# Even layer: products of gates and convolution in 128-column pieces between the steps of its two attentions

## What is computed

```python
q_blocks = jnp.moveaxis(qa.reshape(B, nb, Q_BLOCK, A_HEADS, 2, A_QK), 1, 0)
o = lax.map(lambda qb: diff_attend(qb, k_all, v_all, lam), q_blocks)   # p0 - lam * p1, 768 keys
...
out_a = diff_attention_post(o, subln, lam_init).astype(px.dtype) * jax.nn.silu(ga)
out_b = short_conv(bb, cb, ub, conv_w) * jax.nn.silu(gb)               # b * conv3(c * u)
out_x = jnp.concatenate([out_a, out_b], axis=-1)
...
oc = diff_attend(qc.reshape(B, L, A_HEADS, 2, A_QK), kc, vc, lam)      # context: 256 keys
```

## Time and profile before

| | us |
|---|---|
| median of three runs (lowest, highest) | 1628.0 (1619.35, 1629.15) |
| profiled execution, its own time | 1629.48 |
| its span | 1627.7 |
| busy: PE, DVE, ACT, POOL | 1428.6, 743.7, 661.2, 433.1 |
| attention d, first score to last dc copy | 795.8 to 980.1 |
| first e_ga product to last gc product | 988.5 to 1162.7 |

### The profile page before, as it was taken

One profiled execution on the slowest core, in us unless ns is written; L12 is line 12 of the kernel. 1 busy time (PEld: TensorE's weight loads), 2 busy tenths in 40 slices (PEclk: granted clock), 3 DMA queues, 4 the chain that ended last, 5 costly groups with the idle time before them and its releaser, 6 DMA issues. The chain is left out here.

```text
span 1627.7 us, 20847 instructions
## 1 busy us (share of the span) xinstructions
PE 1428.6 (88%) x7788; PEld 1145.8 (70%) x7788; DVE 743.7 (46%) x1455; ACT 661.2 (41%) x1426; POOL 433.1 (27%) x340
## 2 busy tenths in 40 slices
PE   5999789999999788599899879999795898889986
PEld 4777567776787566586677757888684786777765
DVE  2154875644314222604499887322303603982123
ACT  4435226643422333421477662411224423663323
POOL 2433243430343323122100002323131333112522
PEclk9999899999999899799999989999998899999998
DMA  4212242100333534320000001121222210103341
GB/s 160 85 71 78 104 156 78 53 27 27 130 130 128 195 110 149 117 95 35 26 1 1 2 1 52 52 78 53 85 84 107 87 75 26 47 24 138 122 151 56
DMA packets 23250, 129.98 MB, mean 80 GB/s; under 512 B 2544, under 2 KB 4208, under 8 KB 10608
## 3 DMA queue, kind: packets, MB, share of 16 engines
q1 hardware_dynamic: 16304, 106.10, 18.0%
q10 hardware_dynamic: 6848, 22.55, 3.9%
HBM read 122.35 MB, written 6.29 MB: 79 GB/s over the span
## 5 line engine op out<-in xcount | busy, mean ns | idle before, releaser
L930 POOL TENSOR_TENSOR w_low<-w_raw,w_high 128x512 fp32r<-128x512 f32 x296 | 384.6, 1308 | 1112.7 <-ACT w_high L1017 1112.5
L1017 ACT CAST w_high<-w_raw 128x512 fp32r<-128x512 f32 x296 | 179.2, 620 | 667.9 <-PE psum L564 490.8
L564 PE MATMUL psum<-x_high,w_high 128*128 128x512 f32 (+1 forms) x696 | 285.1, 410 | 18.1 <-DVE k_low L1615 8.9
L564 PE MATMUL psum<-x_low,w_high 128*128 128x512 f32 (+1 forms) x696 | 275.0, 395 | 0.0
L564 PE MATMUL psum<-x_high,w_low 128*128 128x512 f32 (+1 forms) x696 | 274.2, 394 | 0.0
L564 PEld LDWEIGHTS psum<-x_high,w_high 128*128 128x128 f32 (+1 forms) x696 | 132.3, 190 | 59.6 <-issue 26.8
L679 PE MATMUL psum<-k_high,q_masked 128*128 128x256 f32 (+3 forms) x512 | 139.2, 356 | 31.4 <-DVE q_masked L1609 15.6
L564 PE MATMUL psum<-w_high,x_high 128*128 128x512 f32 (+1 forms) x352 | 140.5, 399 | 20.0 <-ACT w_high L1017 12.7
L564 PEld LDWEIGHTS psum<-x_high,w_low 128*128 128x128 f32 (+1 forms) x696 | 131.7, 189 | 30.1
L564 PEld LDWEIGHTS psum<-x_low,w_high 128*128 128x128 f32 (+1 forms) x696 | 132.4, 190 | 21.9 <-issue 0.5
L564 PE MATMUL psum<-w_low,x_high 128*128 128x512 f32 (+1 forms) x352 | 137.8, 391 | 0.0
(11 more groups left out here) (262 smaller groups left out, 2468.3 us busy)
## 6 DMA issues: line engine op xcount, KB each, us to landing
w_raw<-stream SPq DMA_DIRECT2D x98, 1024.0 KB, 4.8
x_kept<-arena ACTq DMA_DIRECT2D x8, 512.0 KB, 4.3
arena<-x_kept ACTq DMA_DIRECT2D x8, 512.0 KB, 6.5
arena<-bias ACTq DMA_DIRECT2D x8, 448.0 KB, 3.3
arena<-rows ACTq DMA_DIRECT2D x6, 512.0 KB, 5.3
arena<-x SPq DMA_DIRECT2D x4, 512.0 KB, 5.2
arena<-x ACTq DMA_DIRECT2D x4, 512.0 KB, 6.0
arena<-ctx ACTq DMA_DIRECT2D x4, 512.0 KB, 4.9
```

The source lines that it names most:

```text
L564: mm = pe.matmul(o, l, r, start=(first and n == 0 and kind != "fc"), stop=(last and n == len(passes) - 1))
L930: pool.tensor_tensor(WL[:, u % ROOM, :], RAW[:, g % 2, u % 4, :], WH[:, u % ROOM, :].bitcast(F32), ALU.subtract).then_inc(w_lo, 1)
L1017: act.copy(WH[:, u % ROOM, :], RAW[:, g % 2, u % 4, :]).then_inc(w_hi, 1)
```

## The change

The five chunks after e_v become 20 slim ones of 128 columns, in the order gate, c, u, b, last gate for each of four column blocks; each is two units, with four k of 128 rows in one unit. `slim` makes a chunk in 16 pieces: eight k for x (three 128x512 matmuls each, bank 6), then eight k for the context (three 128x256 matmuls, bank 7). The two attentions run in one loop over 48 steps on each engine, with four calls of `feed_even` per step, which lay 320 pieces over the first 45 steps, one or two at a time. All transposes use bank 4, all value products bank 5. What ACT and DVE do with a finished chunk stands in their `fed_even`, one step behind PE. The square means come after the loop, and each attention tile is scaled and gated at once. The rows of `w_out` are rolled by 512, so that eo0 starts with the convolution's half. In `dc` ACT now copies out all transposes, where DVE copied half.

```diff
+SLIM = ("e_gate", "e_c", "e_u", "e_b", "e_last")
...
+    + [("e_q", 8), ("e_k", 8), ("e_v", 8)] + [(f"{part}_{j}", 2) for j in range(4) for part in SLIM]
...
+    chunks |= halves("eo", np.roll(a["w_out_2"][0], -512, axis=0)) | halves("oo", a["w_out_2"][1]) | {"dft": dft}
     stream = np.zeros((4 * N_GRANULES, P, 512), f)
     for name, units in UNITS.items():
...
                     for k in range(len(UNITS[chunk])):
                         yield from tiles(chunk, k, X)
+            def slim(chunk):
+                units = UNITS[chunk]
+                for part, x in enumerate((X, C)):
+                    key = (chunk, part)
+                    acc = open_bank(key, 6 + part)
+                    for k in range(NK):
+                        u = units[k // 4]
+                        pe.wait_ge(w_hi, u + 1)
+                        pe.wait_ge(w_lo, u + 1)
+                        w = slice(P * (k % 4), P * (k % 4) + P)
+                        wh, wl = WH[:, u % ROOM, w], WL[:, u % ROOM, w]
+                        hi, lo = x[k]
+                        o = acc[:, 0:hi.shape[-1]]
+                        for n, (l, r) in enumerate(((wh, hi), (wh, lo), (wl, hi))):
+                            mm = pe.matmul(o, l, r, start=k == 0 and n == 0, stop=k == NK - 1 and n == 2)
+                        if k == NK - 1:
+                            fills_bank(mm, key)
+                            closed.append(key)
+                            if part:
+                                unit_done[u] = (bank_full[fills[key][0]], fills[key][1] + 1)
+                        elif part and k == 3:
+                            used[0] += 1
+                            mm.then_inc(w_used, 1)
+                            unit_done[u] = (w_used, used[0])
+                        yield
...
                     next(pieces, None)
                 new = set(unit_done) - before
                 fed[phase].append(max(new) if new else (fed[phase] or [-1])[-1])
+                while closed:
...
             keys = lambda pr, w: (KH[:, pr, 0:w], KL[:, pr, 0:w])
-            attention("d", keys, *pv)
-            attention("dc", keys, *pv)
...
+                    mm = pe.transpose(acc[:, P * (kt - c):P * (kt - c) + P],
+                                      E_P[:, 2 * (i % 2), P * kt:P * kt + P], ident)
+                fills_bank(mm, key)
...
+            pieces = (piece for j in range(4) for part in SLIM for piece in slim(f"{part}_{j}"))
+            n_pieces, n_feeds = 4 * len(SLIM) * 2 * NK, 4 * (len(EVEN) - 3)
+            def feed_even():
+                n = len(fed["e"])
+                feed("e", pieces, n_pieces * (n + 1) // n_feeds - n_pieces * n // n_feeds if n < n_feeds else 0)
+            for s in range(len(EVEN) + 3):
+                if s < len(EVEN):
+                    score_two(s, 0)
+                feed_even()
+                if s < len(EVEN):
+                    score_two(s, 1)
+                feed_even()
+                if 1 <= s <= len(EVEN):
+                    turn_two(s - 1, 0)
+                feed_even()
+                if 1 <= s <= len(EVEN):
+                    turn_two(s - 1, 4)
+                if s >= 3 and s % 2:
+                    values_two((s - 3) // 2)
+                feed_even()
+            for n, i in enumerate(TILE_ORDER):
+                pe.wait_ge(sig("sq"), n + 1)
                 acc = next_bank(("ms", i))
                 fills_bank(pe.matmul(acc[:, :], square("ones_blk"), E_SQ[:, i, :], start=True, stop=True),
                            ("ms", i))
-            for chunk in ("e_ga", "cb", "ub", "bb", "gc"):
-                gemm(chunk, X, C)
             gate_rows(0)
-            mixed = [(BH[:, k, :], BL[:, k, :]) for k in range(4)] + X[4:]
-            mixed_c = [(KH[:, k, 0:L], KL[:, k, 0:L]) for k in range(4)] + C[4:]
+            mixed, mixed_c = X[4:] + X[:4], C[4:] + C[:4]
             gemm("eo0", mixed, mixed_c, ready=lambda k: pe.wait_ge(sig("mix_lo"), 3 * (k // 2) + 3))
             gemm("eo1", mixed, mixed_c)
...
+            def fed_even(s):
+                for chunk, part in closed_in("e", s):
+                    name, j = chunk[:-2], int(chunk[-1])
+                    if name in ("e_gate", "e_last", "e_c"):
+                        ps = filled(act, (chunk, part))[:, 0:L if part else S]
+                    if name == "e_gate":
+                        act.activation((E_GC if part else E_G)[:, j, :], ps, ACT.Sigmoid).then_inc(sig("e_gate_sig"), 1)
+                    if name == "e_last":
+                        if j:
+                            act.wait_ge(sig("e_conv_done"), 2 * j - 1 + part)
+                        act.activation((E_WC if part else E_W)[:, :], ps, ACT.Sigmoid).then_inc(sig("e_last_sig"), 1)
+                    if name == "e_c":
+                        if j:
+                            act.wait_ge(sig("e_conv_in_read"), 2 * j - 1 + part)
+                        frees(act.copy((E_ZC if part else E_Z)[:, :], ps), (chunk, part))
+            for hh in range(2):
...
+            for s in range(len(EVEN) + 3):
+                if s:
+                    high((fed["e"] + [fed["e"][-1]] * 8)[4 * s - 1] + ROOM)
+                exps_even(s, 0)
+                if 2 <= s < len(EVEN) + 2:
+                    turned_even(s - 2, 4)
+                if s:
+                    fed_even(s - 1)
+                if 1 <= s <= len(EVEN):
+                    turned_even(s - 1, 0)
...
+            act.wait_ge(sig("e_conv_done"), 8)
+            high_mixed([(XH[:, 4 + j, :], E_Y[:, j, :]) for j in range(4)],
+                       [(CH[:, 4 + 2 * p:6 + 2 * p, :], E_YC[:, 2 * p:2 * p + 2, :]) for p in range(2)], lambda n: None)
+            ahead("e_last_3")
+            for i in TILE_ORDER:
                 ps = filled(act, ("ms", i))
...
+            def fed_even(s):
+                for chunk, part in closed_in("e", s):
+                    name, j = chunk[:-2], int(chunk[-1])
+                    key, w = (chunk, part), L if part else S
+                    g, y = (E_GC[:, j, :], E_YC[:, j, :]) if part else (E_G[:, j, :], E_Y[:, j, :])
+                    z, last_gate = (E_ZC[:, :], E_WC[:, :]) if part else (E_Z[:, :], E_W[:, :])
+                    if name == "e_c":
+                        continue
+                    ps = filled(dve, key)[:, 0:w]
+                    if name == "e_gate":
+                        dve.wait_ge(sig("e_gate_sig"), 2 * j + part + 1)
+                        frees(dve.tensor_tensor(g, g, ps, ALU.mult), key)
+                    if name == "e_u":
+                        consumed(dve, (f"e_c_{j}", part))
+                        frees(dve.tensor_tensor(z, z, ps, ALU.mult), key)
+                        consumed(dve, key)
+                        convolve(j, z, y, w)
+                    if name == "e_b":
+                        dve.wait_ge(sig("e_conv_in_read"), 2 * j + part + 1)
+                        frees(dve.tensor_tensor(y, y, ps, ALU.mult), key)
+                    if name == "e_last":
+                        consumed(dve, (f"e_b_{j}", part))
+                        dve.wait_ge(sig("e_last_sig"), 2 * j + part + 1)
+                        frees(dve.tensor_tensor(last_gate, last_gate, ps, ALU.mult), key)
+                        consumed(dve, key)
+                        dve.tensor_tensor(y, y, last_gate, ALU.mult).then_inc(sig("e_conv_done"), 1)
...
+                max_even(s, 0)
+                if 1 <= s <= len(EVEN):
+                    name, i = EVEN[s - 1]
+                    of_even(name, norm_d, norm_dc)(i, ATT[name].tile(i))
+                if s:
+                    fed_even(s - 1)
+                max_even(s, 1)
+                for name, first, preps in (("d", 0, preps_d), ("dc", ATT["d"].steps, preps_dc)):
...
+                        preps(*ahead_by)
+                if s - ATT["d"].steps in (-2, -1):
+                    preps_dc(0, s - ATT["d"].steps + 2)
+            dve.wait_ge(sig("e_conv_done"), 8)
...
-            for i, v in enumerate(values):
-                dve.tensor_tensor(E_SQ[:, i, :], v, v, ALU.mult).then_inc(sig("sq"), 1)
-            for i, v in enumerate(values):
+            for i in TILE_ORDER:
+                dve.tensor_tensor(E_SQ[:, i, :], values[i], values[i], ALU.mult).then_inc(sig("sq"), 1)
+            gains = [E_G[:, j, :] for j in range(4)] + [E_GC[:, 2 * p:2 * p + 2, :] for p in range(2)]
+            for i in TILE_ORDER:
                 consumed(dve, ("ms", i))
-                r = E_RS[:, i, :]
+                r, v = E_RS[:, i, :], values[i]
                 link(dve.reciprocal(r, r))
-                dve.scalar_tensor_tensor(v, v, scr(83), r, ALU.mult, ALU.mult).then_inc(sig("subln"), 1)
-            dve.wait_ge(sig("subln"), 6)
+                link(dve.scalar_tensor_tensor(v, v, scr(83), r, ALU.mult, ALU.mult))
+                v = v if i < 4 else pair(v)
+                dve.tensor_tensor(v, v, gains[i], ALU.mult).then_inc(sig("e_gated"), 1)
```

(14 more changed lines are left out.)

181 lines of the change are left out of this document (120 added, 61 removed), and 1 row of the table STREAM.

## The result

The changed kernel takes 1665.97 us (median of 4 runs, 1664.92 to 1667.68), the kernel before 1627.18 (4 runs, 1619.35 to 1629.15): ratio 1.0247, 95% interval 1.0228 to 1.0267. The forecast was 1641 with a range up to 1664. The change makes the kernel slower by 2.5%, nearly three times as much as forecast. Its profiled execution took 1667.68 us, its span 1665.9.

The account below looks back on a forecast made before the run. DVE's chain bounds the attentions, PE the chunks. Work 297.3, interleaving 9.2, transposes 11.6, banks 16.0, other waits 4.5, end 10.5 make a 349.1 us loop; with a 47.0 us tail PE restarts 13 us later: 1641 us, range 1611 to 1664.

Parts of the forecast that it names:

- The tail: Between the loop's last copy and PE's restart: 47.0 us, 22.5 more than before, as reciprocals now stand ahead of eo0.
- Banks 6 and 7: In the loop, a chunk's first piece waits until its bank is read out: 16.0 us (bounds 5 and 25).
- work at full clock: PE's work in the loop, d 114.6, fed dc steps 15.5, pieces 167.2: together 297.3 us, with dc's clock loss gone.
- the interleaving: In the loop, weight matmuls behind float32 ones cost 0.11 us at each of 84 changes: 9.2 us (bounds 0 and 15).
- The transposes' wait: In d, PE waits 0.65 us for a 4.18 us chain in five of nine steps: 11.6 us; none in dc.
- The end of the loop: Three dc steps without pieces at dc's old 2.8 us each, plus last values and copy: 10.5 us.
- The table loads: In the loop, 16 sigmoids bring 32 loads of 1.28 us on ACT; PE waits some 0.5 us, six times.
- The rival that I built on it: Table switches of 2.66 us delay PE in d by up to 20 us in all: 1661 us, chance 0.05.
- The second rival: In the loop, POOL's casts hold up DVE's `norm` ahead of the transposes, 27 us more: 1667 us, chance 0.16.
- The first rival: In the loop, PE loses only 2.3% as in the first layer, waits 7 instead of 32 us: 1616, chance 0.27.
- 51 us of gaps are all that can be filled: In the old attentions, PE's pure work is 133.6 of 184.3 us, leaving 51 us of gaps to fill.
- the three terms: The loop's uncertain terms: interleaving 9.2, banks 6 and 7 16, other waits 4.5 us; nearer bounds give 1629 to 1655.

Follow-up runs that it names:

- e3: The changed kernel without the six reciprocals of the means, nothing in their place: 1645.34 us, ratio 1.0109.
- e2: The changed kernel with the loop's 16 sigmoids written as tanh, so that no table is loaded in its loop: 1646.53 us, ratio 1.0122.
- e4: The changed kernel with no pieces in the attentions' 48 steps, all 320 in 48 further steps: 1770.13 us, ratio 1.088.
- e6: The order of e5 with no pieces in the attentions' steps, all 320 in 48 further steps: 1694.52 us, ratio 1.042.
- e5: The changed kernel with transposes two steps behind the scores and the second map of scores behind them, pieces kept: 1655.74 us, ratio 1.0179.
- e8: The changed kernel with e5's order, e2's tanh, and the modulation ahead of the reciprocals: 1643.01 us, ratio 1.0105.
- e11: e5 and e2 with modulation ahead of reciprocals, four query tiles' square, mean and inverse in dc, eo0's later high parts earlier; all transposes in bank 4: 1631.41 us.
- e12: e11 with the second batch of transposes in bank 5, value products right behind the first map of scores, their copy earlier: 1623.19 us, ratio 0.9983.
- e9: The changed kernel with e5's order, e2's tanh, and the second batch of transposes in bank 5: 1661.96 us, ratio 1.0219.

## Why the prediction was wrong, point by point

**The tail was right**: 47.2 us against 47.0. Reciprocals take 3.35 us, 4.78 a tile; PE is idle 28.1 + 5.3 us; the restart waits for L1993. e3 shows the reciprocals' price, 20 us.

**Banks 6 and 7 were right**: 16.1 against 16.0, the first wait 3.33 where 2 to 3 were forecast.

**The step that failed with most weight is "work at full clock".** The prediction gave the clock behind a wait no term, and took "a clock of 1.0 throughout" as the sign of being right. PE was busy 320.3 us instead of 306.5, half of the loop's miss of 27. The clock was 0.96 in d and 0.98 in the fed dc, up to 12.8 us, and some 11 by the starts. That stretches at the lower level stand right behind waits is read from starts; no run changed the clock alone, so what is left for the interleaving (9.2 forecast, some 12 by this reading) is not shown. Three of the six stretches follow waits for bank 6, whose length the prediction had right.

**"The transposes' wait" failed next**, 11.6 us with the chain fixed at 4.18: 19.3 were measured ahead of the loop's end and 6.9 in it. In d it was 14.4 and most chains had the length forecast; what failed is that all would. DVE's list also holds masks that wait for ACT, and gates and the convolution, which delay the second map's maximum and with it ACT; nine chains were longer. "In dc the chain is shorter than PE's own way" was wrong too: with pieces it cost some 5 us.

**The end of the loop was mis-sized**, 17.7 for 10.5. It was taken at dc's old pace, which had scores of the next step ahead. Here the chain stands bare, three of the last gate's table loads lie in it (1154.13, 1158.00 and 1159.96 on ACT), one wait is 3.70 us, behind a `norm` instruction of 1.54 instead of 0.49 us beside POOL, and the clock is 0.61.

**The table loads** were taken at 1.28 us each, hidden but for six waits of 0.5. Their duration was right, their price was not: e2 gives 19 us for 32 loads, 0.6 each. The Trainium skill (ScalarE: Activation LUTs, "What ACT_TABLE_LOAD costs") gives 2.66 us per switch with a drain; no drain is in these rows, an exponential starts 0.02 us behind the load here too (1016.50 + 1.28, 1017.80). The rival that I built on it, 20 us more, came near the size of e2 by luck and in another way: the loads fill ACT's list ahead of the reads of banks 6 and 7 (7.2 us of waits less in e2) and of the masks (5.2 less at `norm`). I had given it 0.05.

**The second rival** (POOL's casts on `norm`) is true in part: `norm` was 6.4 us longer beside POOL in d and 7.4 in dc, 13.8 us of DVE. Taking each such stretch as far as PE waited behind it, at most 8.4 of the 26.2 us at the transposes come from it (an estimate), not 27. Its number, 1667, is near the 1665.97 measured, but by luck. No run leaves POOL's casts out or moves them, so this rival has no experiment of its own. **The first rival** (PE keeps its pace) fell, and for its own reason against it: there the transposes trail by four steps. e4 and e6 show that the lead decides as long as nothing is laid in; with the pieces it gave 10 us (e5), and none once the table loads were gone (e8). What I did not see is that e4's question, the attentions in the new order without pieces, comes ahead of all others: "51 us of gaps are all that can be filled" took the old order's gaps for the new one's. The new order's attentions are 128 us longer, and the pieces filled their gaps first.

How the rest adds up stays partly open: e5, e2, e11 and e12 remove waits that overlap, so no list of prices per cause adds to the 39 us. What is shown is that lead, table loads, shared bank and tail together are worth 43 us: 34 of them behind the loop and 8 in it, although it then holds four of the six reciprocals.

The range's own sum doesn't come out either: the lower bounds of the three terms (0, 5 and 2) give 1618, not 1629. It decides nothing here.

## What to carry to other kernels

Before filling gaps, ask whether the order that lets the filler in leaves the old work at its old pace: run the new order with nothing laid in. Give each wait the slower stretch that may follow it. A chain's length has to be read with everything that now stands between its links on each engine, since 32 loads of 1.28 us on an engine that is 53% busy still cost 19 us (e2). A bank shared by two uses cost little where its reader had most of a step between them (three waits, 5.5 us, in e12), and a wait each time where they followed each other (16 waits, 24.2 us, in e9). And see what a wait costs in time before pricing its removal.

## What was not expected of the hardware

A wait of 3.33 us on PE was followed by 6 us at 0.43 us per 512 columns instead of 0.23. DVE instructions on 768 columns took 1.90 to 1.93 us instead of 1.02 while POOL wrote its casts, and those two casts took 2.87 us together instead of the usual 1.29 each, so both engines paid. Over the loop this made `norm` 13.8 us longer, and every stretched instruction of `norm` overlaps a cast.
